# Value products with their output turned, and the first gate chunk of the second branch as a dense chunk instead of filler units

## The reference

```python
(q_a, k_c, v_c, k_s, v_s, k_w, v_w, g_nsa, c_q, c_kv, k_r, gate_a, gate_b) = split(rmsnorm(h) @ w_in)
# first family (nsa): 16 heads of 96 in 4 groups, values of 64, three branches
o = gb[..., 0:1] * o_c + gb[..., 1:2] * o_s + gb[..., 2:3] * o_w   # compressed, selected, window
# second family (mla): 16 heads, keys of 64 + 32, values of 64, causal softmax
p = masked_softmax(sc, kpos[None, :] <= t[:, None]);  o = einsum('bhqk,bkhd->bqhd', p, v)
mixed = sigmoid(gate_a) * (o_a @ w_o_nsa) + sigmoid(gate_b) * (o_b @ w_o_mla)
h = h + mixed @ w_out
```

## Time and profile before

| | us |
|---|---|
| median of 3 runs | 2810.18 |
| lowest and highest | 2809.88, 2811.41 |
| the profiled execution | 2811.72 |
| its span, first to last instruction | 2809.9 |

### The profile page before, as it was taken

How to read it: one execution, slowest core, us unless ns; L and a number is a source line. 1 busy time by engine, 2 the same in 40 slices (tenths; PEclk the granted TensorE clock), 3 DMA queues, 4 the chain that set the end, 5 groups by cost and what they waited for, 6 DMA issues and landing times.

```text
span 2809.9 us, 30873 instructions
## 1 busy us (share of the span) xinstructions
PE 2798.4 (100%) x13433; PEld 2342.7 (83%) x13433; DVE 1486.4 (53%) x1187; ACT 1223.4 (44%) x1271; POOL 14.7 (1%) x28
## 2 busy tenths in 40 slices
PE   9999999999999999999999999999999999999999
PEld 7888888888888888888888888888888888888887
DVE  5445654455455445445455674655555445445555
ACT  5435554344554334343344544444433333333453
POOL 0000000000000000000000000000000000000000
PEclk9999999999999999999999999999999999999999
DMA  7745025655555555555555654545555555555555
GB/s 238 217 139 165 31 77 194 195 187 199 183 172 188 195 191 183 195 190 185 194 182 193 209 193 149 181 152 193 200 194 194 192 186 191 194 192 187 177 182 177
DMA packets 256438, 508.17 MB, mean 181 GB/s; under 512 B 8162, under 2 KB 18992, under 8 KB 255408
## 3 DMA queue, kind: packets, MB, share of 16 engines
q1 hardware_dynamic: 254112, 495.61, 53.7%
q0 software_dynamic: 2016, 10.36, 1.2%
q10 hardware_dynamic: 176, 0.23, 0.0%
HBM read 504.08 MB, written 2.10 MB: 180 GB/s over the span
## 4 chain that ended last, share of the span: by engine, by line
PE 99%; DVE 1%; DMA 0%; ACT 0%; SPq 0%; issue 0%; DVEq 0%
PE acc L665 30%; PE acc L666 30%; PE acc L670 30%; PE tb L651 2%; PE acc L914 1%; PE tb L969 1%; PE tb L789 1%; PE tb L933 0%; PE acc L896 0%; PE tb L1152 0%; DMA h<-in_x 0%; PE acc L867 0%; PE acc L864 0%; PE acc L866 0%; PE tb L1142 0%; PE tb L1169 0%
## 5 line engine op out<-in xcount | busy, mean ns | idle before, releaser
L1780 DVE TENSOR_TENSOR wlo<-raw,whi 128x2048 fp32r<-128x2048 f32 (+1 forms) x465 | 1063.7, 2289 | 872.5 <-ACT whi L1325 871.9
L1325 ACT ACTIVATE whi<-raw 128x2048 fp32r<-128x2048 f32 (+1 forms) x465 | 889.3, 1914 | 980.2 <-PE acc L670 791.5
L665 PE MATMUL acc<-whi,ahi 128*128 128x512 f32 (+1 forms) x1968 | 768.1, 391 | 0.4 <-DVE alo L1872 0.4
L666 PE MATMUL acc<-whi,alo 128*128 128x512 f32 (+1 forms) x1968 | 762.4, 388 | 0.0
L665 PE MATMUL acc<-whi,bhi 128*128 128x512 f32 x1528 | 597.0, 391 | 0.1
L666 PE MATMUL acc<-whi,blo 128*128 128x512 f32 x1528 | 594.6, 389 | 0.0
L670 PE MATMUL acc<-wlo,ahi 128*128 128x512 f32 (+1 forms) x1968 | 484.2, 387 | 0.0
L665 PEld LDWEIGHTS acc<-whi,ahi 128*128 128x128 f32 x1968 | 370.9, 188 | 75.4 <-DVE wlo L1869 0.9
L666 PEld LDWEIGHTS acc<-whi,alo 128*128 128x128 f32 x1968 | 370.9, 188 | 74.0
L670 PEld LDWEIGHTS acc<-wlo,ahi 128*128 128x128 f32 x1968 | 367.2, 188 | 75.5
L670 PE MATMUL acc<-wlo,bhi 128*128 128x512 f32 x1528 | 377.8, 389 | 0.0
(11 more groups left out here) (341 smaller groups left out, 1599.8 us busy)
## 6 DMA issues: line engine op xcount, KB each, us to landing
raw<-in_w_ff SPq DMA_DIRECT2D x128, 1024.0 KB, 5.1
raw<-in_w_in SPq DMA_DIRECT2D x119, 1024.0 KB, 5.1
raw<-in_w_gate SPq DMA_DIRECT2D x44, 1024.0 KB, 5.1
raw<-in_w_up SPq DMA_DIRECT2D x44, 1024.0 KB, 5.1
raw<-in_w_down SPq DMA_DIRECT2D x44, 1024.0 KB, 5.1
raw<-in_w_out SPq DMA_DIRECT2D x16, 1024.0 KB, 5.1
raw<-in_w_o SPq DMA_DIRECT2D x16, 1024.0 KB, 5.1
raw<-in_w_ple_gate SPq DMA_DIRECT2D x16, 1024.0 KB, 5.1
```

Of the source, the lines that this page charges most:

```text
L665: nc.tensor.matmul(out_(t), hi[:, kt, tt(t)], whi[:, slot, wc(k)], start=first and k == 0, stop=False)
L666: nc.tensor.matmul(out_(t), lo[:, kt, tt(t)], whi[:, slot, wc(k)], start=False, stop=False)
L1325: nc.scalar.activation(whi[:, g % SPLIT, 0:n_], raw[:, g % RAW, 0:n_], ACT.Copy).then_inc(w_hi, 1)
L1780: V.tensor_tensor(wlo[:, g % SPLIT, 0:n_], raw[:, g % RAW, 0:n_], whi[:, g % SPLIT, 0:n_].bitcast(F32), ALU.subtract).then_inc(w_lo, 1)
```

## The change

- **Value products.** The values become the stationary operand (64 columns) and the transposed probabilities the moving one: per head one product of 256 columns (key tile 0, both query tiles) and one of 128 (key tile 1). The output has value dimensions in partitions, one head of a pair in 0 to 63 and the other in 64 to 127, and queries in columns. The branches of a pair add up in PSUM (`tb[1]`, 256 columns per pair), so one group's results stay there until its last item. The compressed branch's products swap their operands in the same way.
- **Scaling.** As the queries are no longer in partitions, 1/sum and gate are multiplied into the probabilities ahead of their transposes: `scale_of(m-1)` on VectorE, between the maxima of item m and the copy of item m-2. TensorE's `middle_of` waits for `scaled` instead of `exp_done`. `probs_of` does all of the compressed branch's normalization. VectorE's `end_of` is gone.
- **Output.** At the end of a group ScalarE copies the turned outputs (`o_out`) to `qkv` or `qm`; TensorE's first value products of the next group wait for that. `o_rounded` (ScalarE) and `o_rest` (VectorE) make `bhi` and `blo` from them in four quarters, two of them in the last steps of attention and two in the gate chunk. The four `turn`s are gone, so GpSimd's fetch of `mem` waits for 10 turns instead of 14. Some buffers move within the same region.
- **Gate chunk.** The filler units, their half conversions and their plan are gone. SyncE fetches the same 1024 x 256 blocks as four groups of 512 x 512, and `chunk(ahi, alo)` runs them densely behind attention, ahead of the two half chunks, as a chunk of its own (`C_GB0`), with the sigmoid in its copy. All later chunk numbers grow by one, so the two accumulators swap roles (`xa`, `xb`).

```diff
@@ TensorE
-                        pe.wait_ge(exp_done, it["n"] + 1)
+                        pe.wait_ge(scaled, it["n"] + 1)
...
-                        for n in range(2):
-                            hd = 4 * it["g"] + 2 * it["pair"] + n
-                            for t in range(TT):
-                                bs = [b for b, (tq, _) in enumerate(BLOCKS[f]) if tq == t]
-                                o = tb[1][:, (n * TT + t) * dv:(n * TT + t + 1) * dv]
-                                for b in bs:
-                                    last = nc.tensor.matmul(o, probT[:, p % 2, n, b * P:(b + 1) * P],
-                                                            value_of(it, hd, BLOCKS[f][b][1]),
-                                                            start=b == bs[0], stop=b == bs[-1])
+                        o = pairs_at(it["pair"])
+                        for tk in range(TT):
+                            for n in range(2):
+                                hd = 4 * it["g"] + 2 * it["pair"] + n
+                                last = nc.tensor.matmul(o[n * DV:(n + 1) * DV, tk * P:SEQ], value_of(it, hd, tk),
+                                                        probT[:, p % 2, n, 2 * tk * P:(2 + tk) * P],
+                                                        start=first and tk == 0, stop=it["br"] != 1 and tk == 1,
+                                                        skip_group_check=True)
...
-                    fill(FILL.get(m, 0))
...
-            turn(pieces(qkv, 0))
-            fill(2)
-            turn(pieces(qkv, 4 * P), into=acc[0])
-            chunk(bhi, blo, 8, need={0: 1, 1: 1},
-                  hook={1: lambda: (attended(), turn(pieces(qm, 0)))})
-            chunk(bhi, blo, 8, kt0=8, need={0: 1, 1: 0},
-                  hook={0: lambda: turn(pieces(qm, 4 * P), lambda: pe.wait_ge(fill_free, 2))})
+            chunk(ahi, alo)
+            for half in range(2):
+                chunk(bhi, blo, 8, kt0=8 * half,
+                      hook={j: lambda n=2 * half + j: pe.wait_ge(o_lo, n + 1) for j in range(2)})
@@ ScalarE
+            def o_out(m):
+                it = items[m]
+                n = group_of(it)
+                act.wait_ge(pv_done, it["u"] + 1)
+                for t in range(TT):
+                    src = tb[1][:, 0:COLS].rearrange("p (k t i) -> p k t i", k=2, t=TT)[:, :, t, :]
+                    dst = (qkv if it["fam"] == "nsa" else qm)[:, t, 2 * it["g"] * P:2 * (it["g"] + 1) * P]
+                    last = nc.scalar.activation(dst.rearrange("p (k i) -> p k i", i=P), src, ACT.Copy)
+                last.then_inc(o_done, 1)
...
             def attend():
...
-                    fill_step(m)
+                    if m - DEPTH in calls[0] and group_end(m - DEPTH):
+                        o_out(m - DEPTH)
...
+                    if m in (calls[0][-1] - 1, calls[0][-1]):
+                        o_rounded(m - calls[0][-1] + 1)
...
+            o_out(calls[0][-1])
+            block_of(4, {1: lambda: o_rounded(2), 2: lambda: o_rounded(3)},
+                     ev=lambda: take(lambda t: gb0[:, t, :], ACT.Sigmoid, R_X))
@@ VectorE
+            def scale_of(m):
...
+                dve.wait_ge(exp_done, it["n"] + 1)
...
+                link(V.reciprocal(rinv[:, 0, :], sums[:, p % 4, :]))
+                linked()
...
+                for t in range(TT):
+                    x = prob[:, p % 2, :, t * P:(2 * t + 1) * P]
+                    last = V.tensor_tensor(x, x, r[:, :, t:t + 1].to_broadcast([P, 2, (t + 1) * P]), ALU.mult)
+                last.then_inc(scaled, 1)
...
-                    for step, k in ((end_of, m - deep), (middle_of, m - deep + 1)):
+                    for step, k in ((scale_of, m - 1), (middle_of, m - deep + 1)):
...
+                    if m in (ms[-1], ms[-1] + 1):
+                        o_rest(m - ms[-1])
```

More of the change, by code:

```diff
@@ L422, in build, with group_of, group_start, group_end @@
         C_QKV, C_GA0, C_UQ, C_UK, C_UV = 0, 9, 10, 13, 15
[L423 to L427, removed]
+        C_GB0, C_MIX, C_OUT, C_KX, C_QX, C_XO = 17, 18, 32, 36, 37, 38
+        C_FF, C_IN2, C_O2, C_GUD, C_PLE, C_PG = 42, 74, 88, 92, 126, 130
+        G_XV, FILL_KT, FILL_COLS = 111, 8, 256
         ga0 = qkv[:, :, O_CQ:O_CQ + COLS]
         gb0 = qkv[:, :, O_KC:O_KC + COLS]
[L431 to L453, removed]
+        def group_of(it):
+            return it["g"] + (0 if it["fam"] == "nsa" else KVH)
+        def group_start(m):
+            it = items[m]
+            return it["kind"] == "attn" and it["pair"] == 0 and it["br"] in (0, 1)
+        def group_end(m):
+            it = items[m]
+            return it["kind"] == "attn" and it["pair"] == 1 and it["br"] in (0, 2)
+        xa, xb = acc[C_QX % 2], acc[1 - C_QX % 2]
         def fronts(m):
@@ L542, in gates @@
                 chunks(wml, at, 0, 8)
-            for half in range(2):
-                for kt in range(0, KT, FILL_KT):
-                    group(win, O_GB + half * FILL_COLS, kt, FILL_KT, FILL_COLS)
+            chunks(win, O_GB, 0)
             chunks(wna, 0, 0, 8)
@@ L948, in end_of @@
                         return
-                    u = it["u"]
-                    if u:
-                        pe.wait_ge(o_done, u)
+                    pairs_at = lambda n: tb[1][:, n * SEQ:(n + 1) * SEQ]
                     if it["kind"] == "cmp":
                         pe.wait_ge(cmp_pts, it["n"] + 1)
-                        for t in range(TT):
-                            last = nc.tensor.matmul(tb[1][:, t * HPG * DV:(t + 1) * HPG * DV],
-                                                    pcT[:, t, :], bdv[:, it["g"], :], start=True, stop=True)
+                        for pair in range(2):
+                            last = nc.tensor.matmul(pairs_at(pair), bdv[:, it["g"], pair * P:(pair + 1) * P],
+                                                    pcT[:, :, :].rearrange("p t i -> p (t i)"),
+                                                    start=False, stop=False, skip_group_check=True)
                         last.then_inc(pv_done, 1)
@@ L2093, in conv_half, with o_rest @@
-            def conv_half(half, n):
-                g, part = w.n["group"], slice(half * GSIZE // 2, (half + 1) * GSIZE // 2)
-                if half:
-                    dve.wait_ge(w_hi, w.val("group", 1))
-                else:
-                    dve.wait_ge(w_hi_half, n)
-                ins = V.tensor_tensor(wlo[:, g % SPLIT, part], raw[:, g % RAW, part],
-                                      whi[:, g % SPLIT, part].bitcast(F32), ALU.subtract)
-                if half:
-                    ins.then_inc(w_lo, 1)
-                w.n["group"] += half
+            def o_rest(n):
+                dve.wait_ge(o_hi, n + 1)
+                for t in range(TT):
+                    src = (qkv if n < 2 else qm)[:, t, n % 2 * COLS:(n % 2 + 1) * COLS]
+                    at = (slice(None), slice(4 * n, 4 * n + 4), slice(t * P, (t + 1) * P))
+                    last = V.tensor_tensor(blo[at], src.rearrange("p (k i) -> p k i", i=P), bhi[at].bitcast(F32),
+                                           ALU.subtract)
+                last.then_inc(o_lo, 1)
@@ L2197, in _ @@
             conv(1)
-            x_max(1, acc[0])
+            x_max(1, xa)
             x_probs(0, tb[1])
```

191 lines of the change are left out of this document (65 added, 126 removed).

## The result

| | before | after |
|---|---|---|
| median of the runs beside each other | 2810.24 us (6 runs, 2809.84 to 2813.46) | 2822.82 us (6 runs, 2821.45 to 2825.04) |
| ratio after / before | | 1.0041, 95% interval 1.003 to 1.0052 |
| profiled execution, span | 2811.72, 2809.9 us | 2823.55, 2821.5 us |
| mean granted clock | 0.997 | 0.995 |
| attention, first preparation to next section | 134.1 us | 128.9 us |

The change makes the kernel slower by 12.6 us, 0.4%. The two sections together grow by 11.2 us (172.5 against 161.3), the span by 11.6, so nearly all of the difference lies between the first preparation and the end of the half chunks.

A forecast was written before the change was run, and what follows sets the result against it. TensorE was taken to bound the kernel at 99% of the chain, with fillers covering waits in attention. Attention 126.8 - 134.1 plus 16.3 behind it gave +9.0 us on the 2810.18 median: 2819 us, range 2811 to 2830.

The forecast's parts named there:

- rival A: Attention's value products: the two heads' products overlap in their column halves, 0.75 us per item, 2815 us in all; chance 0.30.
- The idle time: Sign on TensorE in attention: fewer than 14 us idle would make the forecast wrong; 22.6 us was forecast.
- The work behind attention: TensorE after attention: 8 dense groups of 5.44 us, 43.5 us where 27.2 were, so +16.3 us.
- The price of V: An item's turned value products on TensorE: 1.31 us if serial, against 1.33 before; bounds 0.75 and 1.51.
- Each product is two instructions in the same half: Argument on the value products, raised against the two heads' products overlapping in their column halves.
- the walk: Adding three engine queues through attention in program order: 126.0 us, with 29.4 start, 20.1 per group, 4.80 per second-family item.
- its 0.8 of correction: Added to attention's computed time, since the same addition gave 133.3 us for the kernel before against 134.1 measured.
- Rival B: The clock falls in attention: 2822 us with one spell at the start, up to 2840 with one per group; chance 0.17.
- rival C: VectorE's copies of item m-2 come early enough: attention 102 us, 2794 in all, deciding at 117.8; chance 0.08.
- The scaling ahead of the copy: VectorE's queue in attention: scaling of 1.45 us (1.25 without a gate) stands ahead of the copy that V needs.
- A wait for probT, about 20 us in total: Sign in attention: a V or its weight load waits for the transposed probabilities, about 20 us in total.
- fill the time in which a V waits for the copies: Claim on attention's 32 filler units, 0.80 us each: they also cover value products' waits for VectorE's copies.

The follow-up runs named there:

- experiment 2: Changed kernel with the value products issued head by head (four of the first head, then four of the second) instead of alternating: 2823.08 us, ratio 1.0044.
- experiment 10: Changed kernel with both heads' value products in the same column half, the second head's in an unused bank and not read: 2825.46 us, ratio 1.0049.
- 11: Changed kernel with 128 instead of 64 value columns as the stationary operand, each head's output in its own bank: 2826.54 us, ratio 1.0053.
- experiment 8: Changed kernel with unused 512-column products in idle time, 13 at attention's start and 8, 4, 2 before the last three value products: 2818.02 us, ratio 1.0022.
- experiment 1: Changed kernel with 13 products of unused result put in the idle gap at attention's start, ahead of item 5's scores: 2821.96 us, ratio 1.0037.
- experiment 5: Changed kernel with VectorE's copy of item m-2 put ahead of the scaling of item m-1: 2819.22 us, ratio 1.0027.
- experiment 7: Changed kernel with the scaling's multiplications cut to one column per block, every wait kept: 2817.03 us, ratio 1.0018.
- 4: Changed kernel with filler units, their half conversions and plan put back, and no dense gate chunk: 2802.29 us, ratio 0.997.

## Why the prediction was right in sign and size, and where it failed

- **The signs.** The median fell in the stated range, but two of the prediction's own signs went against the forecast: value products under 1 us were rival A's sign, and a granted clock under 1.00 in attention was named as one that would make the forecast wrong. The idle time passed its sign (20.8 us, over 14).
- **The work behind attention: right.** +16.3 us forecast, +16.5 measured (43.67 less 27.20). The dense chunk took 21.91 us (forecast 21.8), and the rounding of the output and the conversions stayed covered.
- **The price of V: wrong.** The step "V = 0.86 + 0.45 = 1.31 us, so nothing is won per item if the two heads' products go one after the other" failed: they don't go one after the other. V is 0.80, next to the lower bound of 0.75 of rival A. "Each product is two instructions in the same half" was no argument against: even when one head's products are all issued ahead of the other's, the two heads overlap (experiment 2), and 1.44 in one half and 1.36 at full width (10, 11) show where 0.80 comes from. The Trainium skill, page "TensorEngine Tiling (Array Packing)", section "Tiling Modes", says that different tiles can load and multiply in parallel; experiment 10 against after agrees, 1.44 to 0.80. A serial price of 1.31 was about right as such, 0.05 to 0.13 low.
- **What the cheaper V is worth: right, and small.** 24 x 0.51 = 12.2 us less work than forecast should shorten attention by 3.6 us only (the walk has 122.1 with 0.75, about 122.4 with 0.80, with its 0.8 of correction 123.2, against 126.8). With the clock held it took 123.9 (experiment 8). That the rest of the 12.2 turns into waits fits experiment 10, where 15.4 us more of V made attention 4.1 us longer.
- **The clock: its price was left out of the sum.** Rival B's single spell at the start came, at the forecast gap (3.7 us forecast, 3.31 measured). It costs 5.0 us (29.16 against 34.1 in experiment 1; 4.9 in experiment 8), where B had put 3.4. The length was what B had wrong: a mean of 0.58 over the 8 us of the earlier trace rows is 6.8 us at half the clock, and here it was at half for 13.7 us, over all four stretches from 278 to 294. In them TensorE lost 0.38 x 3.01 + 0.50 x 3.33 + 0.50 x 4.00 + 0.32 x 4.00 = 6.1 us of full-speed work, of which 5.0 reached the end of attention. The Trainium skill, page "TensorE: Matmul & The Clock Gate", section "HAM oscillation", says that idle gaps between bursts bring the clock down. The trace agrees at the start, 0.62 and 0.50 behind the gap. It doesn't give the whole: at the end a gap of 2.07 us was followed by a fall in experiment 1, and one of 2.06 us by none in after. What decides it is open.
- **Two misses cancelled.** 126.8 - 3.6 + 5.0 = 128.2 against 128.9 measured. The 2819 forecast and the 2822.8 measured are this 2.1, the 0.2 of the work behind attention, 0.4 of the span outside the two sections (11.6 less 11.2), and the rest spread between runs and profiled execution. The likeliest description would have been rival A with one spell: 2815 + 5 = 2820.
- **The walk: right in its parts.** With V at 0.75 to 0.80 it gives 28.9 us for the start (29.16 in experiment 1, without the spell), 19.6 per group (19.9: starts 303.85, 323.74, 343.63) and 4.74 per item of the second family (4.84). The idle time at the end was forecast at 4.35 us in three gaps, and is 3.93 (2.06, 1.20 and 0.67). Its idle time is added up wrongly: the parts (8.1, 3 x 3.2, 4 x 0.33, 4.35) make 23.4 us and not 22.6. The time of 126.0 and the forecast do not use that figure; the 14.4 us that rival C needs with a V of 1.31 would be 15.2.
- **The scaling ahead of the copy: right as a cause, not the whole.** It costs 3.7 us by its place (experiment 5), and its two multiplications 5.9 in all (experiment 7). "A wait for probT, about 20 us in total" came to 9.2 us in V itself and 8.0 in its weight loads, which partly name the same idle time; 7.2 us of idle time hang on exponentials instead.
- **The fillers: the main cause, as forecast.** The forecast said that they "fill the time in which a V waits for the copies". Experiment 8 against 4 puts this cover at 15.7 us, and after against experiment 8 puts the clock, which they also held, at 4.8. The sum, 20.5 us, is the right column against the left of the table for turned products, and must be, as the two differences share experiment 8. For the old products it is 17.9, and there too the start ran 13.7 us at the lower clock.

Rival C (faster) is out: with the clock held, attention is 123.9 us and not under 117.8.

## What to carry to other kernels

Work of another chunk that is dealt out between dependent steps isn't overhead, even where it delays each step: count the waits that it covers before you make it a dense block of its own, and price the idle time that it leaves at the clock which that idle time may bring. When an edit has two parts, price each alone; here the half that was right (turned products, -8.7 us beside fillers) was hidden by the half that was not (+20.5). A cheaper instruction on the engine with the most work gives only what the queue of the engine that feeds it lets through: 12.2 us of work less gave 3.6 in the walk (15.4 more cost 4.1 in experiment 10), and the order of two steps on VectorE, which costs no work at all, gave as much (3.7).

## What was not expected of the hardware

- Products of 64 stationary columns in the two column halves overlap whatever the order in which they are issued: 0.80 us for eight of them alternating or head by head, 1.44 in one half, 1.36 to 1.41 with 128 stationary columns. A product issued later in the other half starts ahead of one issued earlier (experiment 2).
- Held at one sparse place, the clock can fall at the next: experiment 1 had 1.00 at the start and 0.62, 0.50, 0.60 at the end, where after had 1.00. With products in the gaps of both ends it was 1.00 at both, at no cost in time.
- Removing the scaling did not help the clock: 0.50 from 278 to 290 in experiment 7, with TensorE's start as sparse as in after.
